# Experts add weighted rows to the output by indirect DMA; SyncE loads the down weights; the combining stage goes

## The reference

```python
ids, wts = route(hn, ...)                  # two experts and two weights for each row
# rows sorted by expert, each expert padded to whole blocks of 128 rows
xb = xf[row_tok].reshape(n_blocks, 128, -1)
yb = (silu(xblk @ w_gate[e]) * (xblk @ w_up[e])) @ w_down[e]     # for each block
out = zeros.at[row_tok].add(yb * row_w[:, None])                 # back to rows, weighted
h = h + out
```

## Time and profile before

| | us |
|---|---|
| median of 3 runs (3883.65 to 3895.85) | 3886.66 |
| the profiled execution | 3893.31 |
| its span, first to last instruction | 3891.7 |
| TensorE busy in the span | 3223.6 (83%) |
| mean granted TensorE clock | 0.906 of 2.4 GHz |
| `experts`, from its start to its barrier | 2855 to 3788 |
| `combine` | 3788 to 3891.7 |

### The profile page before, as it was taken

One profiled execution on the slowest core, in us unless ns is written; L12 is line 12 of the kernel. 1 busy time (PEld: TensorE's weight loads), 2 busy tenths in 40 slices (PEclk: granted clock), 3 DMA queues, 4 the chain that ended last, 5 costly groups with the idle time before them and its releaser, 6 DMA issues. The chain is left out here.

```text
span 3891.7 us, 62377 instructions
## 1 busy us (share of the span) xinstructions
PE 3223.6 (83%) x22582; PEld 2700.3 (69%) x22583; DVE 1889.6 (49%) x2769; ACT 1486.6 (38%) x2958; POOL 398.2 (10%) x393
## 2 busy tenths in 40 slices
PE   7999999899969996568599966888339999999980
PEld 7999999788858885334277743677237778778860
DVE  5242356455534555311256631332436876686734
ACT  5112354355545554123123212443035655454520
POOL 1000000000000000040000010111131211121113
PEclk9999999899979998678699986988569999999995
DMA  4333332234441111164233322223158977796849
GB/s 163 121 110 140 140 110 99 86 115 127 148 127 35 64 56 51 51 200 135 98 117 114 115 95 89 90 95 98 37 193 305 340 283 269 273 350 228 293 180 340
DMA packets 309939, 591.64 MB, mean 152 GB/s; under 512 B 80597, under 2 KB 136323, under 8 KB 309230
## 3 DMA queue, kind: packets, MB, share of 16 engines
q1 hardware_dynamic: 250846, 365.54, 28.6%
q0 software_dynamic: 47776, 196.29, 13.7%
q10 hardware_dynamic: 11136, 27.27, 1.9%
HBM read 462.13 MB, written 160.44 MB: 160 GB/s over the span
## 5 line engine op out<-in xcount | busy, mean ns | idle before, releaser
L136 PE MATMUL pj_pu<-pj_w,pj_nT 128*128 128x256 f32 (+3 forms) x1088 | 306.8, 282 | 0.0
L137 PE MATMUL pj_pu<-pj_w,pj_nT 128*128 128x256 f32 (+3 forms) x1088 | 305.9, 281 | 0.0
L138 PE MATMUL pj_pu<-pj_w,pj_nT 128*128 128x256 f32 (+3 forms) x1088 | 305.2, 281 | 0.0
L137 PEld LDWEIGHTS pj_pu<-pj_w,pj_nT 128*128 128x128 f32 (+1 forms) x1088 | 202.1, 186 | 0.0
L138 PEld LDWEIGHTS pj_pu<-pj_w,pj_nT 128*128 128x128 f32 (+1 forms) x1088 | 202.0, 186 | 0.0
L136 PEld LDWEIGHTS pj_pu<-pj_w,pj_nT 128*128 128x128 f32 (+1 forms) x1088 | 201.6, 185 | 0.1
L3076 ACT ACTIVATE ex_gate<-ex_gate_raw 128x2048 fp32r<-128x2048 f32 x64 | 119.1, 1909 | 204.0 <-DMA ex_gate_raw<-in_w_gate 116.8
L716 ACT ACTIVATE att_prob<-att_score,att_res 128x256 f32<-128x256 f32 (+1 forms) x384 | 127.6, 443 | 143.9 <-DVE att_res L752 143.9
L3130 DVE TENSOR_TENSOR ex_gate<-ex_gate_raw,ex_gate 128x2048 fp32r<-128x2048 f32 x64 | 143.8, 2288 | 72.1 <-ACT ex_gate L3076 60.9
L136 PE MATMUL pj_pu<-pj_nT,pj_w 128*128 128x384 f32 (+2 forms) x480 | 175.3, 365 | 0.0
L136 PE MATMUL ex_py<-ex_down,ex_hT 128*128 128x512 f32 x384 | 152.7, 398 | 26.2 <-DVE ex_hT L131 26.2
(11 more groups left out here) (580 smaller groups left out, 8168.6 us busy)
## 6 DMA issues: line engine op xcount, KB each, us to landing
ex_gate_raw<-in_w_gate SPq DMA_DIRECT2D x32, 2048.0 KB
ex_up_raw<-in_w_up SPq DMA_DIRECT2D x32, 2048.0 KB, 11.2
ex_down_raw<-in_w_down POOLq DMA_DIRECT2D x32, 2048.0 KB, 8.4
tmp_yb<-ex_y ACTq DMA_DIRECT2D x48, 512.0 KB, 7.1
out_win_k<-in_cache_k POOLq DMA_DIRECT2D x8, 2032.0 KB, 13.1
out_win_v<-in_cache_v POOLq DMA_DIRECT2D x8, 2032.0 KB, 14.2
tmp_att<-att_res POOLq DMA_DIRECT2D x48, 264.0 KB, 4.4
pout_att<-tmp_att SPq DMA_DIRECT2D x16, 792.0 KB, 7.4
```

What stands on the lines that cost most here:

```text
L136: pe.matmul(out, ah, bh, start=start, stop=False)
L137: pe.matmul(out, ah, bl, start=False, stop=False)
L138: return pe.matmul(out, al, bh, start=False, stop=stop)
```

## The change

`combine` goes. `memory_attention` stores h2 straight into the output `y`, which has a spare tile behind the last row. `route` scatters pairs (row number, weight) instead of row numbers, over a list that is filled beforehand with spare rows of weight 0. In `experts`, ScalarE multiplies by the row's weight while it copies y out of PSUM, and GpSimd adds the block to the output with an indirect DMA (`compute_op=ALU.add`), one at a time: before it issues the add of a block it waits for y of that block and for the add of the block before. GpSimd gathers one block further ahead than before. The down load moves from GpSimd to SyncE, behind the gate and up loads of the same expert. The stores of y to `yb` and the zeros go.

```diff
@@ memory_attention, SyncE
-                    sp.dma_start(t["h2"][i], h2[:]).then_inc(E["h2_out"], 16)
+                    sp.dma_start(t["y"][i], h2[:]).then_inc(E["h2_out"], 16)
+                sp.wait_ge(E["consts_in"], 80)
+                for n in ("hn", "y"):
+                    sp.dma_start(t[n][NT], gf[:]).then_inc(E["spare_out"], 16)
@@ route, VectorE
+                own.then(dve.tensor_copy(tokw[:, :, :, 1].bitcast(F32), wts[:]))
                 dve.tensor_copy(dsti[:], dst[:]).then_inc(E["placed"], 1)
@@ experts, SyncE
                 def load(i, u, b):
-                    sp.sem_inc(E["zero_out"], 16)
                     with sp.If(read(sp, 2, b, 1)):
                         e = read(sp, 0, b, NE - 1)
                         r = began(sp, b)
-                        for piece, name in (("g", "w_gate"), ("u", "w_up")):
+                        for piece, name in (("g", "w_gate"), ("u", "w_up"), ("d", "w_down")):
                             sp.wait_ge(E[piece + "_split"], 2 * r)
                             sp.dma_start(raw[piece][:], t[name][e].rearrange("(k p) c -> p k c", p=P)).then_inc(E[piece + "_in"], 16)
-                def nothing(b):
-                    sp.dma_start(t["yb"][b], zero[:]).then_inc(E["zero_out"], 16)
-                sp.wait_ge(E["zero_ok"], 1)
@@ experts, GpSimd
                 def work(i, u, b):
-                    pool.wait_ge(E["x_turned"], b + 1)
-                    gather(u, b + 2, i + 2)
-                    with pool.If(read(pool, 2, b + 1, 1)):
-                        e = read(pool, 0, b + 1, NE - 1)
-                        pool.wait_ge(E["d_split"], 2 * began(pool, b + 1))
-                        pool.sem_inc(E["seen"], 1)
-                        load_down(e)
-                    pool.wait_ge(E[f"x_in{u}"], 16 * i + 32)
+                    v = 1 - u
+                    pool.wait_ge(E["x_turned"], b + 2)
+                    gather(v, i + 2 + u)
+                    pool.wait_ge(E[f"x_in{v}"], 16 * i + 32 + 16 * u)
                     pool.sem_inc(E["seen"], 1)
-                    load_rows(u, b + 4)
+                    load_rows(v, b + 5)
+                    pool.wait_ge(E["y_ok"], 2 * b + 4)
+                    pool.wait_ge(E["added"], 16 * b + 16)
+                    pool.sem_inc(E["y_free"], 1)
+                    load_place(v, b + 1)
+                    pool.indirect_dma_start(t["y"].rearrange("n p d -> (n p) d"), bass.IndirectOffsetOnAxis(ap=place[:, u, 0:1].bitcast(U32), axis=0),
+                                            y[:, u, :], None, compute_op=ALU.add).then_inc(E["added"], 16)
@@ experts, ScalarE
-                    act.wait_ge(E[f"y_out{u}"], i * 16 + 16)
+                    act.wait_ge(E["y_free"], b + 1)
+                    act.wait_ge(E[f"place_in{u}"], 16 * i + 16)
                     for n in range(2):
-                        act.activation(y[:, u, 512 * n:512 * n + 512], py[:, n, :], ACT.Copy).then_inc(E["y_ok"], 1)
-                    act.wait_ge(E["y_ok"], 2 * b + 4)
-                    act.dma_start(t["yb"][b], y[:, u, :]).then_inc(E[f"y_out{u}"], 16)
+                        act.activation(y[:, u, 512 * n:512 * n + 512], py[:, n, :], ACT.Copy, scale=place[:, u, 1:2].bitcast(F32)).then_inc(E["y_ok"], 1)
@@ the stage combine (57 lines) and its name in STAGES are removed
```

More of the change, by code:

```diff
@@ L53 @@
 NBLK += NBLK % 2
-NBX = NBLK + 4
+NBX = NBLK + 8
 class Stage:
@@ L2596, in _ @@
                     sp.wait_ge(E[e], NT * 16)
+                sp.wait_ge(E["spare_out"], 32)
             @block.gpsimd
@@ L2820, in route @@
         pt = s.ps("total", [P, 2, 512])
-        names = "loaded zero_ok zeroed own exp_ok sums_ok placed planned scattered saved".split()
+        names = "loaded filled own exp_ok sums_ok placed planned scattered saved".split()
         E = dict(zip(names, s.sem(*names)))
@@ L2954, in experts @@
         plan = s.sb("plan", [1, 3, NBX + 1], I32)
-        idx = s.sb("idx", [P, 2, 1], I32)
+        idx = s.sb("idx", [P, 2, 2], I32)
+        place = s.sb("place", [P, 2, 2], I32)
         xb = s.sb("xb", [P, 2, D])
@@ L2969, in experts @@
         names = ("consts_in seen idx_in0 idx_in1 x_in0 x_in1 g_in u_in d_in g_hi u_hi d_hi g_split u_split d_split x_turned x_hi x_ok "
-                 "gate_mm up_mm sg_ok hh_ok h_turned h_hi h_ok y_mm y_ok y_out0 y_out1 zero_ok zero_out").split()
+                 "gate_mm up_mm sg_ok hh_ok h_turned h_hi h_ok y_mm y_ok place_in0 place_in1 added y_free").split()
         E = dict(zip(names, s.sem(*names)))
@@ L2978, in began, with blocks @@
             return read(eng, 1, b, NE)
-        def blocks(eng, body, beyond=None):
+        def blocks(eng, body):
             used = read(eng, 0, NBX, NBLK)
@@ L2986, in blocks @@
                         body(i, u, 2 * i + u)
[L2987 to L2990, removed]
             return (used + 1) // 2
@@ L3012, in load @@
                         r = began(sp, b)
-                        for piece, name in (("g", "w_gate"), ("u", "w_up")):
+                        for piece, name in (("g", "w_gate"), ("u", "w_up"), ("d", "w_down")):
                             sp.wait_ge(E[piece + "_split"], 2 * r)
                             sp.dma_start(raw[piece][:], t[name][e].rearrange("(k p) c -> p k c", p=P)).then_inc(E[piece + "_in"], 16)
-                def nothing(b):
-                    sp.dma_start(t["yb"][b], zero[:]).then_inc(E["zero_out"], 16)
-                sp.wait_ge(E["zero_ok"], 1)
-                blocks(sp, load, nothing)
-                sp.wait_ge(E["zero_out"], 16 * NBLK)
+                blocks(sp, load)
             @block.gpsimd
             def _(pool):
-                pool.memset(zero[:], 0.0).then_inc(E["zero_ok"], 1)
                 rows = t["i_rows"].rearrange("(n p) o -> n p o", p=P)
@@ L3031, in load_rows, with load_place, gather @@
                     pool.dma_start(idx[:, u, :], rows[b]).then_inc(E[f"idx_in{u}"], 16)
-                def gather(u, b, nth):
+                def load_place(u, b):
+                    pool.dma_start(place[:, u, :], rows[b]).then_inc(E[f"place_in{u}"], 16)
+                def gather(u, nth):
                     pool.wait_ge(E[f"idx_in{u}"], 16 * nth)
@@ L3045, in _ @@
                 for u in range(2):
-                    gather(u, u, 1)
+                    gather(u, 1)
+                load_place(0, 0)
+                pool.dma_start(place[:, 1, :], rows[1]).then_inc(E["added"], 16)
                 for u in range(2):
@@ L3104, in work @@
                     act.wait_ge(E["y_mm"], b + 2)
-                    act.wait_ge(E[f"y_out{u}"], i * 16 + 16)
+                    act.wait_ge(E["y_free"], b + 1)
+                    act.wait_ge(E[f"place_in{u}"], 16 * i + 16)
+                    act.sem_inc(E["seen"], 1)
                     for n in range(2):
-                        act.activation(y[:, u, 512 * n:512 * n + 512], py[:, n, :], ACT.Copy).then_inc(E["y_ok"], 1)
-                    act.wait_ge(E["y_ok"], 2 * b + 4)
-                    act.dma_start(t["yb"][b], y[:, u, :]).then_inc(E[f"y_out{u}"], 16)
[L3111 to L3114, removed]
+                        act.activation(y[:, u, 512 * n:512 * n + 512], py[:, n, :], ACT.Copy, scale=place[:, u, 1:2].bitcast(F32)).then_inc(E["y_ok"], 1)
+                blocks(act, work)
             @block.vector
@@ L3283 @@
 STAGES = [project, attend_prompt, delta_prompt, delta_net_sample, window_sample_to_out,
-          memory_attention, route, experts, combine]
+          memory_attention, route, experts]
 def delta_consts(name, chunk, rows, levels):
@@ L3433 @@
     out = {n: r[f"out_{n}"] for n in OUTPUTS}
-    flat = {n: out[n].reshape((ROWS, -1)) for n in ("k", "v", "y")}
+    flat = {n: out[n].reshape((-1, out[n].shape[-1])) for n in ("k", "v", "y")}
     return (flat["y"][:SEQ].reshape(1, SEQ, D), flat["y"][SEQ:SEQ + NS].reshape(DEC_B, DEC_T, D),
```

100 lines of the change are left out of this document (22 added, 78 removed).

## The result

The changed kernel takes 3914.38 us (median of 6 runs, 3906.26 to 3917.10), the kernel before 3891.27 us (6 runs, 3883.65 to 3895.85): ratio 1.0057, 95% interval 1.0042 to 1.0072, so it is slower by 0.6%. The forecast was 3879 us, 7.4 us faster, with a range of 3852 to 3912. The profiled execution took 3914.78 us, its span is 3913.2 us, that of before 3891.7: +21.5 us. The combining stage is gone, and more than it cost was lost again in the experts stage.

What follows compares the result with a forecast made beforehand. It took VectorE, TensorE and DMA to be near their limits in one-block experts, and TensorE to set the pace in two-block ones. Removal -99.4, move +89 and clock +3 gave -7.4 on 3886.7, hence 3879 us, range 3852 to 3912.

Steps and rivals of the forecast that it cites:

- removal: End of the span: the combining stage goes and a last add takes its place, -99.4 us, bounds 91 to 102.
- move, eleven places: Where one one-block expert follows another: late gate load costs 8.1 us each, 89 us in all, bounds 81 to 120.
- clock, and all other edits: TensorE's clock after stalls, at the ends of 6 runs of one-block experts: 3 us, 0 to 20; other edits nothing.
- base of 3886.7: Median time of the kernel before, in us, from which the forecast took off 7.4 us.
- (1): Experts stage: the late gate load is hidden, the move is free, only the removal counts, 3787 us; chance 0.08.
- (2): GpSimd's ring: adds landing in over 14.5 us set the pace, two-block experts over 37 us, 3938 us; chance 0.06.
- Rival (3): One-block runs: adds and gathers slow the loop, step 30 us, cold clock at each run's end, 3927 us; chance 0.12.
- T + 13.7: One-block runs: gate load landed 13.7 us after T, the end of a down split, by landings of 8.4 and 5.1.
- The other edits, at nothing: VectorE's extra copy, spare stores, weight multiplication and GpSimd's waits for y were together taken to cost nothing.
- nothing is later: Where every expert has two blocks, down is split ahead of the next gate anyway, so the move costs nothing.
- TensorE the pace at 71.3 of 73 us: Two experts of two blocks, 2961 to 3034 us: TensorE busy 71.3 of 73 us was taken to set the pace.

Runs made afterwards that it cites:

- e_move: The kernel before, with only the down load moved from GpSimd to SyncE behind gate and up, no adds, combining stage kept: 4001.68 us, before 3896.68.
- e_order: The changed kernel, with SyncE issuing its loads in the order in which VectorE splits them: 3830.38 us.
- e_read_ahead: The changed kernel, with SyncE reading the plan for the next gate load ahead of its wait for the down split: 3915.58 us.
- b_hoist: The kernel before, with only VectorE's two reads of the plan moved ahead of the product of silu and up: 3883.65 us, before 3894.23.
- e_hoist: The changed kernel, with VectorE's two plan reads for the down split moved to the start of its body: 3876.65 us.
- e_order_hoist: The changed kernel, with SyncE's loads in the order of VectorE's splits and VectorE's plan reads at the body's start: 3794.56 us.

## Why the prediction was wrong

By its own terms, in the profiled executions:

| term | predicted | measured |
|---|---|---|
| removal: from the start of the last copy of y to the end | -99.4 (-91 to -102) | 15.0 - 111.9 = -96.9 |
| move, eleven places | +89 (81 to 120) | 303.6 - 208.7 = +95.0 |
| clock, and all other edits | +3 (0 to 20) | 20 other steps +24.4, last expert +1.7: +26.1 |
| start: the first down split | 0 | 2896.3 - 2898.9 = -2.6 |
| sum | -7.4 | +21.5 |

In medians it is +23.1 (3914.4 - 3891.3) against -7.4. The forecast of 3879 us went by a base of 3886.7, and beside the changed kernel that one took 3891.3, so 4.6 of the 35 us by which the time was missed lie in the base, and the rest in the terms. The first down split lies at 2893 to 2905 us in the eleven kernels, so a few us of difference there say nothing.

**The removal** was right, within its bounds, with two errors of opposite sign: the last add landed 6.0 us after its issue began, where 0.95 + 8.2 were taken, and 6.1 us lie behind the landing, where 1.2 were taken; the drain of GpSimd was not in the sum. **The rivals** (1) and (2) fell: the one-block stretches did not keep 19 us, and no add came near 14.5 us (at most 10.1). Yet the sign that was given for rival (2) came true, two-block experts over 37 us, by another mechanism. Rival (3) came nearest in total (3927), for a wrong reason: the step inside the runs is 27.6 us and not 30. Of (1) the trace shows both halves: the rule in the Trainium skill, DMA: Bandwidth & Descriptors, Issuing engines are not separate DMA queues, holds for the transfer (the same down load lands in 8.4 us, the median, issued by GpSimd, and in 8.9 issued by SyncE in e_move), and the order of waits on the issuing engine costs 95 us all the same. (Rows 7 alone, which set two different loads side by side, did not show that yet.)

**The move** was right in mechanism and place (e_move, e_order) and 6 us short in size: 8.6 us a place against 8.1. The part of it that was off is the landing: the gate was to be there at T + 13.7 (8.4 + 5.1 are 13.5), with the second load at 418 GB/s, and came at T + 14.9 on average. The same rows had ScalarE get up 7.4 us after gate and not 5.1. ScalarE then took 6.3 us to the upper half of down where 7.0 were taken, so a part of the error cancels. I had put SyncE's reads of the plan at nothing, which e_read_ahead bears out to 0.3 us, though they take 2 us.

**The step that failed** is the one headed "The other edits, at nothing", and the sentence on two-block experts, "nothing is later". It is true of SyncE's loads (e_move: 36.62 us). But an add has been issued some 2 to 4 us before VectorE reads the plan ahead of the down split, and a read there takes up to 1.4 us in place of 0.3; TensorE waits for that split in each two-block expert. I had priced what GpSimd waits for and when the add lands, and not what stands beside it on other engines. In the kernel before the read was already on the path there (b_hoist: 36.57 to 36.05), in a stretch in which I had called TensorE the pace at 71.3 of 73 us: the 1.7 us that I left open were, by b_hoist, this wait. The 9 and 5 steps that start at a two-block expert gained 10.7 + 8.1 = 18.8 us, and e_hoist takes all of that back and more. The other 5.5 us, in the six steps that end a run, come with the move (5.0 in e_move); each of these steps begins with 2 to 4 us at half clock in the change, so they are what the term for the clock was for, and it held. The last expert's 1.7 us are a stretch at half clock as well; in the ten other kernels it took what it took before, to 0.1 us.

**The clock** in two-block experts was not forecast: TensorE's wait grew from about 1.3 us in the kernel before to 2.3 to 2.5 at eleven places, and some 3.5 us at half clock followed at five of them, where steps of 37.6 became 39.3. Why not at the other six stays open. Where the read is off the path (e_hoist) the wait and the loss are both gone.

The bounds of all terms together were given as 3862 to 3918; added up as they stand they are 3866 to 3936. That 3914 lies within them is luck: that room belongs to terms that held, and what was missing was a term, and a term that is not in the sum has no bound in the range.

## What to carry to other kernels

Before a load moves to another engine, write down the order in which its buffers come free, and issue in that order: here the move cost 95 us or 12, by the order of three lines. Then look at what the engine that sets the pace waits for in its last per cents, since a stretch at 98% busy can still hold a wait that something new makes longer. A register read from SBUF that stands between a product and the next engine's input belongs ahead of the wait, where it cost nothing here, above all when a store is issued a few us before it.

## What the hardware showed that was not expected

- A read of one number into a register of VectorE took 0.3 us (at most 0.58 in the kernel before), and up to 1.54 us when it began 2.3 to 4.0 us after the issue of an indirect add of 0.5 MB; in e_move a read 1.1 us after the issue of a plain store by ScalarE took 1.30.
- Two loads of 2 MB on one queue, issued 0.7 or 2.7 us apart, had the second ready 14.6 and 14.9 us after the first's issue (means of eleven), in one pair in a stretch at 302 to 376 GB/s and not 418.
- An indirect add of 128 rows of 4 KB landed in 6.9 us (median; 9.2 in e_order_hoist), an indirect write of the same rows in 5.3.
